# Root-mean-square factors of the two latents computed with tokens on partitions

## The chip, the cores and the metric

The kernel runs on one core of a Trainium2 chip. The metric is the device time of one launch in microseconds. Three runs of the kernel before gave 1781.26, 1781.75 and 1782.9 us, so the median is 1781.75 us.

## The reference

A decoder trunk of two layers works on 256 tokens with 2048 features, in float32. Layer one is a causal pooling mixer and a SwiGLU feed-forward block (FFN, 5632 hidden features); layer two is multi-head latent attention (16 heads) and another FFN; a root-mean-square norm (RMSNorm) ends it. What the change touches is the low-rank part of the attention:

```
y  = x * rsqrt(mean(x*x) + eps) * gain            # rms_norm
kv = rms_norm(x, kv_in_norm) @ w_kv_a             # 512 latent + 64 rotary features
c_kv = rms_norm(kv[..., :512], kv_latent_norm)    # then @ w_kv_b: keys, values of 16 heads
k_pe = apply_rope(kv[..., 512:], cos, sin)
q  = rms_norm(rms_norm(x, attn_norm) @ w_q_a, q_latent_norm) @ w_q_b   # 512 latents, 16 heads
```

Two norms follow each other here: the norm of x gives one factor per token (the same for q and kv, since only the gains differ), and each latent has a norm of its own over its 512 features.

## The kernel before

Activations lie transposed in the on-chip memory: features on the 128 partitions, the 256 tokens along the free dimension. x is 16 tiles of 128x256. Each weight is float32 and comes in by DMA in chunks of 512 to 704 KB (`raw`, 8 slots). ScalarE (ACT) copies a chunk to the rounded type fp32r (`w_hi`), VectorE (DVE) writes the rest (`w_lo`), and TensorE (PE) multiplies: for each 128x128 weight tile one matmul of `w_hi` with 512 columns (the high and low halves of the activations side by side) and one of `w_lo` with the 256 high columns (`product3`, lines 404 and 405). The kpe stage and the heads use three matmuls of 256 columns (`product_one`, lines 412 to 414).

The order of every engine's work is written out by hand. Each engine runs its own program, in order, and they meet only at semaphores. Along x there is no norm factor in the matmul operand: the operand is x times the gain, and the factor of each token is applied behind the matmul. The attention's low-rank part is these stages on PE:

- **qa**, four tiles (m = 0 to 3) of 16 weight tiles each, operand `xg`: the query latent. After m = 0, `sum_over_partitions(2)` sums the squares of x over the partitions: a matmul of an all-ones 128x128 matrix with `square_sum` (float32, 256 columns), so that each partition gets the sum of each token. ACT takes the root of the 128x256 result (`root_of`, line 820), DVE its reciprocal (`rstd_of`, line 1203).
- **kva**, four tiles, operand `xk`: the key/value latent. After m = 1, `sum_over_partitions(3)` does the same for the squares of the query latent.
- **kpe**, one tile: the shared rotary key. Between its weight tiles 7 and 8, `latent_stats` sums the squares of the key/value latent (lines 568 and 570).
- **heads**, eight pairs of heads; the first query projections follow kpe at once, the first key projection waits for the key/value latent.

For each pair of latent tiles DVE adds the two halves of the product (`lat_add`, line 1359, into `sums`), multiplies by x's factor `rstd` (`lat_scale`, line 1365, into `lat_raw`), and GpSimd (POOL) squares it and adds it up (`latent_squares`, lines 1630 and 1631). DVE itself squares the last pair of the key/value latent (lines 1419 and 1420). When the factor of the latent norm is there (`lat_rstd_of`, line 1369), DVE multiplies the four tiles by it (`lat_norm`, line 1376), ACT writes gain times that as the high half (`lat_split`, line 963) and DVE the low half (line 1381). `key_scale` (line 1427) multiplies the rotary key by x's factor; it stands between the two multiplications of `lat_norm`. ACT's four partition swaps (`rope_swap`, line 995) and `rope_cos` (line 1456) on DVE then free the PSUM bank that the first key projection writes.

Of the kernel before, what the change touches and what calls it, by code (L numbers as in the profile page):

```python
# [142 lines left out]
def trunk(nc, xT, positions, consts, bands, gains, pool_w, w_kv_a, w_k_pe, w_q_a, w_kv_k, w_kv_v, w_q_nope, w_q_pe,  # L143
          w_o, w_gate, w_up, w_down, w_last, final_gain, out):
    with ExitStack() as ctx:
# [51 lines left out]
        lat_rstd = at("lat_rstd", [P, SEQ], F32, scratch_at + 6 * KB)  # L197
# [71 lines left out]
        lat_sum = sem("lat_sum")  # L269
# [40 lines left out]
        KV, Q = 0, 1  # L310
        INIT = 4
# [88 lines left out]
        def _(pe):  # L400
# [58 lines left out]

            pe.wait_ge(init_ready, INIT)  # L460
# [92 lines left out]
            for m in range(LT):  # L553
                long_tile(CHUNK["qa"] + 2 * m, TILE["qa"] + m, xg, TILES,
                          each=(lambda kt: pe.wait_ge(xg_ready, DT + kt + 1)) if m == 0 else None)
                if m == 0:
                    sum_over_partitions(2)

            for m in range(LT):
                long_tile(CHUNK["kva"] + 2 * m, TILE["kva"] + m, xk, TILES,  # L560
                          each=(lambda kt: pe.wait_ge(xg_ready, 2 * DT + kt + 1)) if m == 0 else None)
                if m == 1:
                    sum_over_partitions(3)
            def latent_stats():

                pe.wait_ge(squares_added, squares_before(5))
                pe.wait_ge(root_ready, 4)
                pe.matmul(ps[:, STATS, 0:SEQ], ones[:, :], square_sum[:, :], start=True, stop=False)
                pe.wait_ge(pair_squared, 1)
                pe.matmul(ps[:, STATS, 0:SEQ], ones[:, :], lat_square[:, 0, :], start=False,  # L570
                          stop=True).then_inc(stats_summed, 1)

            long_tile(CHUNK["kpe"], TILE["kpe"], xk, TILES, each=lambda kt: latent_stats() if kt == TILES else None,
# [222 lines left out]
        def _(sc):  # L796
# [161 lines left out]

            def lat_split(which, number, col):
                for t in range(LT):  # L960
                    if t % 2 == 0:
                        sc.wait_ge(lat_scaled, 2 * number + t // 2 + 1)
                    nc.scalar.activation(latent[:, which, t, 0:SEQ], lat_raw[:, t, :], ACT.Identity,
# [3 lines left out]
            for w in range(3):  # L967
                split(n0 + w + SPLIT_SLOTS)
                xk_some(2)
                if w == 1:  # L970
                    root_of(3, D_MODEL)
            lat_pair("qa", 0)
            for w in range(3, 7):
                split(n0 + w + SPLIT_SLOTS)
                xk_some(2)
# [7 lines left out]
            root_of(4, LATENT)  # L983
# [14 lines left out]
            root_of(5, LATENT)  # L998
# [160 lines left out]
        def _(ve):  # L1159
# [192 lines left out]
            def lat_add(name, m):  # L1352
# [4 lines left out]
                if m > 0:  # L1357
                    ve.wait_ge(lat_sum, 1 if name == "qa" else 3)
# [431 lines left out]
```

## Time and profile before

| | |
|---|---|
| median of three runs | 1781.75 us |
| profiled execution | 1783.35 us |
| its span | 1781.4 us |
| PE busy | 1766.1 us (99%) |
| DVE busy | 1137.8 us (64%) |
| ACT busy | 915.5 us (51%) |
| POOL busy | 113.2 us (6%) |
| granted TensorE clock, mean | 0.999 of full speed |
| stages qa, kva, kpe and the first pair of heads | about 780 to 850 us |

The span runs from the first to the last instruction of one execution that the hardware profiler recorded; busy time is the time in which an engine had an instruction running. PE counts matmuls and PEld the weight loads, which overlap them. All times below are microseconds from the start of the span.

### The profile page before, as it was taken

The numbers are of one execution on the slowest core, as the hardware profiler recorded it, in microseconds if no ns is written. First come the engines' busy times: TensorE is split into PE (matmuls) and PEld (weight loads), VectorE is DVE, ScalarE is ACT, GpSimd is POOL, SyncE is SP. The second block draws the span as 40 slices with busy tenths as digits, with TensorE's granted clock in tenths as the row PEclk, the third lists the DMA queues.
The fourth block names the chain that finished last, engine by engine and source line by source line (L and its number), as shares of the span: only waits on it lengthen the run. The fifth ranks groups of instructions, "written<-read, shape, count | busy, mean of one in ns | idle before, by whom it ended". The sixth has DMA issues, their size and how long they took to land.

```text
span 1781.4 us, 29177 instructions
## 1 busy us (share of the span) xinstructions
PE 1766.1 (99%) x10376; PEld 1562.5 (88%) x10376; DVE 1137.8 (64%) x1456; ACT 915.5 (51%) x1176; POOL 113.2 (6%) x129
## 2 busy tenths in 40 slices
PE   9999999999999999999999999999999999999998
PEld 5888888888888888888999888888888888888886
DVE  4866666556666666668997776666655566666553
ACT  5766664334444444455775456666533344445433
POOL 2200000000000001123112420000000000000000
PEclk9999999999999999999999999999999999999999
DMA  6555557545555566544444555555665455556641
GB/s 250 198 190 189 190 189 238 193 158 173 188 188 188 188 224 199 174 152 138 142 154 154 189 189 188 189 188 188 221 204 177 156 189 188 190 190 223 225 147 71
DMA packets 85008, 328.26 MB, mean 184 GB/s; under 512 B 9568, under 2 KB 10336, under 8 KB 84832
## 3 DMA queue, kind: packets, MB, share of 16 engines
q1 hardware_dynamic: 84816, 326.57, 54.6%
q10 hardware_dynamic: 144, 1.05, 0.1%
q8 instruction: 30, 0.49, 0.1%
q14 instruction: 18, 0.15, 0.0%
HBM read 325.48 MB, written 2.10 MB: 184 GB/s over the span
## 4 chain that ended last, share of the span: by engine, by line
PE 97%; DVE 2%; ACT 0%; DMA 0%; issue 0%; POOL 0%; SPq 0%; ACTq 0%; POOLq 0%; DVEq 0%
PE ps L404 57%; PE ps L405 30%; PE ps L475 2%; PE ps L412 1%; PE ps L413 1%; PE ps L414 1%; PE ps L765 1%; PE ps L763 1%; PE ps L764 1%; DMA raw<-pool_w 0%; DVE w_lo L1199 0%; PE ps L598 0%; PE ps L599 0%; PE ps L600 0%; POOL square_sum L1672 0%
## 5 line engine op out<-in xcount | busy, mean ns | idle before, releaser
L1199 DVE TENSOR_TENSOR w_lo<-raw,w_hi 128x1024 fp32r<-128x1024 f32 (+2 forms) x564 | 737.5, 1309 | 421.0 <-ACT w_hi L814 418.7
L404 PE MATMUL ps<-xg,w_hi 128*128 128x512 f32 x2880 | 999.5, 390 | 0.5 <-issue 0.5
L814 ACT ACTIVATE w_hi<-raw 128x1024 fp32r<-128x1024 f32 (+2 forms) x565 | 632.0, 1120 | 552.5 <-PE ps L405 538.2
L405 PE MATMUL ps<-xg,w_lo 128*128 128x256 f32 x2880 | 812.1, 282 | 0.0
L404 PEld LDWEIGHTS ps<-xg,w_hi 128*128 128x128 f32 x2880 | 540.4, 188 | 113.8 <-issue 0.6
L405 PEld LDWEIGHTS ps<-xg,w_lo 128*128 128x128 f32 x2880 | 544.3, 189 | 0.1
L404 PE MATMUL ps<-act,w_hi 128*128 128x512 f32 x1320 | 458.0, 390 | 0.0
L405 PE MATMUL ps<-act,w_lo 128*128 128x256 f32 x1320 | 372.2, 282 | 0.0
L404 PEld LDWEIGHTS ps<-act,w_hi 128*128 128x128 f32 x1320 | 247.7, 188 | 51.9
L405 PEld LDWEIGHTS ps<-act,w_lo 128*128 128x128 f32 x1320 | 249.5, 189 | 0.0
L1279 DVE TENSOR_TENSOR sums<-ps,cross 128x512 f32<-128x512 f32 x88 | 60.9, 692 | 95.5 <-ACT cross L891 95.5
L891 ACT ACTIVATE cross<-ps 128x512 f32<-128x512 f32 x88 | 52.6, 598 | 120.6 <-PE ps L405 120.5
L404 PE MATMUL ps<-heads,w_hi 128*128 128x512 f32 x256 | 89.1, 391 | 0.0
L1630 POOL TENSOR_TENSOR square<-x 128x256 f32 (+1 forms) x32 | 33.2, 1039 | 765.2 <-DVE x L1300 765.2
L405 PE MATMUL ps<-heads,w_lo 128*128 128x256 f32 x256 | 72.2, 282 | 0.0
L1299 DVE TENSOR_TENSOR x<-ps,x 128x256 f32 (+1 forms) x76 | 32.1, 422 | 54.9 <-PE ps L405 54.9
L1283 DVE TENSOR_TENSOR sums<-sums,rstd 128x512 f32<-128x512 f32 x88 | 60.9, 692 | 3.0
L894 ACT ACTIVATE gate_act<-sums 128x256 f32<-128x256 f32 x88 | 36.8, 418 | 46.0 <-DVE sums L1283 45.8
L826 ACT ACTIVATE xg<-x,gain 128x256 fp32r<-128x256 f32 (+1 forms) x48 | 23.4, 508 | 66.5 <-DVE x L1300 62.1
L404 PEld LDWEIGHTS ps<-heads,w_hi 128*128 128x128 f32 x256 | 48.1, 188 | 9.9
L405 PEld LDWEIGHTS ps<-heads,w_lo 128*128 128x128 f32 x256 | 48.4, 189 | 0.0
L412 PE MATMUL ps<-latent,w_hi 128*128 128x256 f32 x160 | 45.2, 283 | 2.5 <-DVE gate_act L1456 2.3
(196 smaller groups left out, 1227.7 us busy)
## 6 DMA issues: line engine op xcount, KB each, us to landing
raw<-w_gate SPq DMA_DIRECT2D x176, 512.0 KB, 3.2
raw<-w_up SPq DMA_DIRECT2D x176, 512.0 KB, 3.2
raw<-w_down SPq DMA_DIRECT2D x120, 704.0 KB, 4.1
raw<-w_o SPq DMA_DIRECT2D x32, 512.0 KB, 3.2
raw<-w_last SPq DMA_DIRECT2D x11, 512.0 KB, 3.2
raw<-pool_w SPq DMA_DIRECT2D x8, 512.0 KB, 12.0
raw<-w_q_a SPq DMA_DIRECT2D x8, 512.0 KB, 3.3
raw<-w_kv_a SPq DMA_DIRECT2D x8, 512.0 KB, 3.2
```

What stands on the lines that cost most here:

```text
L404: pe.matmul(ps[:, bank, :], w_hi[:, s, j * P:(j + 1) * P], moving, start=start, stop=False)
L405: return pe.matmul(ps[:, bank, 0:SEQ], w_lo[:, s, j * P:(j + 1) * P], moving[:, 0:SEQ], start=False, stop=stop)
L412: pe.matmul(dst, w_hi[:, s, j * P:(j + 1) * P], moving[:, 0:SEQ], start=start, stop=False)
L475: mm = pe.matmul(ps[:, 4 + 2 * (g % 2) + s, :], x_pool[:, GT * g + kt, s * P:(s + 1) * P], raw[:, c, j * GT * P:(j + 1) * GT * P], start=( ...
L814: nc.scalar.activation(dst, src, ACT.Copy).then_inc(hi_ready, 1)
L891: nc.scalar.activation(cross[:, :, :], ps[:, bank:bank + 2, SEQ:], ACT.Copy).then_inc(cross_ready, 1)
L894: nc.scalar.activation(gate_act[:, :], sums[:, 0, :], ACT.Silu).then_inc(gate_ready, 1)
L1199: nc.vector.tensor_tensor(lo, src, hi.bitcast(F32), ALU.subtract).then_inc(lo_ready, 1)
L1279: nc.vector.tensor_tensor(sums[:, :, :], ps[:, bank:bank + 2, 0:SEQ], cross[:, :, :], ALU.add).then_inc(evacuated, 2)
L1283: nc.vector.tensor_tensor(sums[:, :, :], sums[:, :, :], r, ALU.mult).then_inc(sums_ready, 1)
L1299: step(nc.vector.tensor_tensor(xd, ps[:, b, 0:SEQ], xd, ALU.add))
L1630: step(nc.gpsimd.tensor_tensor(square[:, :], src, src, ALU.mult))
```

## The change

Three things change. The sums over the partitions are turned round: the squares are now the stationary operand (a 128x128 slice, so that tokens come out on the partitions) and two columns of ones the moving one (`token_sums`), for each half of the tokens. The root and the reciprocal are taken of two columns (`tok`), and PE writes the factors back to all partitions by multiplying a column, repeated 128 times as the stationary operand, with the identity (`spread`). And `lat_scale` is gone: the latents stay unscaled until `lat_norm`, whose factor is now the product of x's factor and the latent's. The root of a latent's norm is taken with x's factor squared over 512 as its scale (`X_SCALE`), one activation for each half of the tokens. ACT copies x's spread factor from PSUM to `rstd` for the rotary key. `spread` stands in PE's order in front of weight tile 8 of qa's tile 1, of weight tile 8 of kva's tile 2, and of weight tile 13 of kpe. The first pair of the key/value latent now stays in `sums`.

```diff
@@ -194,7 +194,7 @@
         lat_raw = at("lat_raw", [P, LT, SEQ], F32, scratch_at)
-        lat_rstd = at("lat_rstd", [P, SEQ], F32, scratch_at + 6 * KB)
+        tok = at("tok", [P, 9, 2], F32, scratch_at + 6 * KB)
         lat_square = at("lat_square", [P, 2, SEQ], F32, scratch_at + 4 * KB)
@@ -266,7 +266,10 @@
         pos_landed = sem("pos_landed")
-        lat_sum = sem("lat_sum")
+        tok_squared = sem("tok_squared")
+        lat_root = sem("lat_root")
+        spread_done = sem("spread_done")
+        rstd_copied = sem("rstd_copied")
         lat_scaled = sem("lat_scaled")
@@ -308,6 +311,16 @@
         KV, Q = 0, 1
+        X_ROOT, X_RSTD, X_SCALE, LAT_TOK = 0, 1, 2, 3
+        def lat_pair_of(which, m):
+            return sums[:, :, :] if (which, m) == (KV, 0) else lat_raw[:, m:m + 2, :]
+        def lat_tile_of(which, t):
+            return sums[:, t, :] if which == KV and t < 2 else lat_raw[:, t, :]
         INIT = 4
@@ -456,6 +469,23 @@
+            def token_sums(k, parts):
+                for s in range(2):
+                    for n, part in enumerate(parts):
+                        mm = pe.matmul(ps[:, STATS, 2 * s:2 * s + 2], part[:, s * P:(s + 1) * P], ones[:, 0:2],
+                                       start=(n == 0), stop=(n == len(parts) - 1))
+                mm.then_inc(stats_summed, 1)
+            def spread(k, row):
+                pe.wait_ge(rstd_ready, k)
+                for s in range(2):
+                    mm = pe.matmul(ps[:, STATS, SEQ + s * P:SEQ + (s + 1) * P],
+                                   tok[:, row, s:s + 1].broadcast_to([P, P]), const[:, C_IDENT:C_IDENT + P],
+                                   start=True, stop=True)
+                mm.then_inc(spread_done, 1)
@@ -551,26 +581,44 @@
             for m in range(LT):
-                long_tile(CHUNK["qa"] + 2 * m, TILE["qa"] + m, xg, TILES,
-                          each=(lambda kt: pe.wait_ge(xg_ready, DT + kt + 1)) if m == 0 else None)
+                def each_qa(kt, m=m):
+                    if m == 0:
+                        pe.wait_ge(xg_ready, DT + kt + 1)
+                    if (m, kt) == (1, TILES):
+                        spread(3, X_RSTD)
+                long_tile(CHUNK["qa"] + 2 * m, TILE["qa"] + m, xg, TILES, each=each_qa)
                 if m == 0:
-                    sum_over_partitions(2)
+                    pe.wait_ge(squares_added, squares_before(3))
+                    pe.wait_ge(root_ready, 2)
+                    token_sums(3, (square_sum,))
             for m in range(LT):
-                long_tile(CHUNK["kva"] + 2 * m, TILE["kva"] + m, xk, TILES,
-                          each=(lambda kt: pe.wait_ge(xg_ready, 2 * DT + kt + 1)) if m == 0 else None)
+                def each_kva(kt, m=m):
+                    if m == 0:
+                        pe.wait_ge(xg_ready, 2 * DT + kt + 1)
+                    if (m, kt) == (2, TILES):
+                        spread(4, LAT_TOK + 2)
+                long_tile(CHUNK["kva"] + 2 * m, TILE["kva"] + m, xk, TILES, each=each_kva)
                 if m == 1:
-                    sum_over_partitions(3)
-            def latent_stats():
-                pe.wait_ge(squares_added, squares_before(5))
-                pe.wait_ge(root_ready, 4)
-                pe.matmul(ps[:, STATS, 0:SEQ], ones[:, :], square_sum[:, :], start=True, stop=False)
-                pe.wait_ge(pair_squared, 1)
-                pe.matmul(ps[:, STATS, 0:SEQ], ones[:, :], lat_square[:, 0, :], start=False,
-                          stop=True).then_inc(stats_summed, 1)
-            long_tile(CHUNK["kpe"], TILE["kpe"], xk, TILES, each=lambda kt: latent_stats() if kt == TILES else None,
+                    pe.wait_ge(squares_added, squares_before(4))
+                    pe.wait_ge(root_ready, 3)
+                    pe.wait_ge(rstd_copied, 1)
+                    token_sums(4, (square_sum,))
+            def each_kpe(kt):
+                if kt == TILES:
+                    pe.wait_ge(squares_added, squares_before(5))
+                    pe.wait_ge(root_ready, 4)
+                    pe.wait_ge(lat_root, 1)
+                    pe.wait_ge(lat_scaled, 2)
+                    pe.wait_ge(pair_squared, 1)
+                    token_sums(5, (square_sum, lat_square[:, 0, :]))
+                if kt == TILES + 5:
+                    spread(5, LAT_TOK + 5)
+            long_tile(CHUNK["kpe"], TILE["kpe"], xk, TILES, each=each_kpe,
                       product=product_one)
@@ -956,11 +1004,19 @@
+            def lat_root_of(number):
+                sc.wait_ge(stats_summed, 4 + number)
+                sc.wait_ge(tok_squared, 1)
+                for s, done in enumerate((lat_root, root_ready)):
+                    nc.scalar.activation(tok[:, LAT_TOK + 3 * number, s:s + 1], ps[:, STATS, 2 * s:2 * s + 1], ACT.Sqrt,
+                                         bias=eps[:, :], scale=tok[:, X_SCALE, s:s + 1]).then_inc(done, 1)
             def lat_split(which, number, col):
...
                         sc.wait_ge(lat_scaled, 2 * number + t // 2 + 1)
-                    nc.scalar.activation(latent[:, which, t, 0:SEQ], lat_raw[:, t, :], ACT.Identity,
+                    nc.scalar.activation(latent[:, which, t, 0:SEQ], lat_tile_of(which, t), ACT.Identity,
                                          scale=gain[:, col + t, :]).then_inc(lat_hi, 1)
@@ -968,8 +1024,13 @@
                 if w == 1:
-                    root_of(3, D_MODEL)
+                    sc.wait_ge(stats_summed, 3)
+                    sc.wait_ge(rstd_ready, 2)
+                    nc.scalar.activation(tok[:, X_ROOT, :], ps[:, STATS, 0:4:2], ACT.Sqrt, bias=eps[:, :],
+                                         scale=1.0 / D_MODEL).then_inc(root_ready, 1)
             lat_pair("qa", 0)
+            sc.wait_ge(spread_done, 1)
+            nc.scalar.activation(rstd[:, :], ps[:, STATS, SEQ:], ACT.Copy).then_inc(rstd_copied, 1)
             for w in range(3, 7):
@@ -980,7 +1041,7 @@
             split(n0 + 11 + SPLIT_SLOTS)
-            root_of(4, LATENT)
+            lat_root_of(0)
             lat_split(Q, 0, G_LQ)
@@ -995,7 +1056,7 @@
-            root_of(5, LATENT)
+            lat_root_of(1)
@@ -1354,32 +1415,31 @@
                 ve.wait_ge(cross_ready, crossed[0])
-                if m > 0:
-                    ve.wait_ge(lat_sum, 1 if name == "qa" else 3)
-                nc.vector.tensor_tensor(sums[:, :, :], ps[:, t % 4:t % 4 + 2, 0:SEQ], cross[:, :, :],
+                which = Q if name == "qa" else KV
+                nc.vector.tensor_tensor(lat_pair_of(which, m), ps[:, t % 4:t % 4 + 2, 0:SEQ], cross[:, :, :],
                                         ALU.add).then_inc(evacuated, 2)
...
-            def lat_scale(m):
-                r = rstd[:, :].rearrange("p (o t) -> p o t", o=1).broadcast_to([P, 2, SEQ])
-                nc.vector.tensor_tensor(lat_raw[:, m:m + 2, :], sums[:, :, :], r, ALU.mult).then_inc(lat_sum, 1)
             def lat_rstd_of(number):
-                ve.wait_ge(root_ready, 4 + number)
-                nc.vector.reciprocal(lat_rstd[:, :], root[:, :]).then_inc(rstd_ready, 1)
-                ve.wait_ge(rstd_ready, 4 + number)
+                k, row = 4 + number, LAT_TOK + 3 * number
+                ve.wait_ge(lat_root, number + 1)
+                ve.wait_ge(root_ready, k)
+                step(nc.vector.reciprocal(tok[:, row + 1, :], tok[:, row, :]))
+                nc.vector.tensor_tensor(tok[:, row + 2, :], tok[:, row + 1, :], tok[:, X_RSTD, :],
+                                        ALU.mult).then_inc(rstd_ready, 1)
...
-                r = lat_rstd[:, :].rearrange("p (o t) -> p o t", o=1).broadcast_to([P, 2, SEQ])
+                r = ps[:, STATS, SEQ:].rearrange("p (o t) -> p o t", o=1).broadcast_to([P, 2, SEQ])
+                ve.wait_ge(spread_done, 2 + number)
                 for m in (0, 2):
-                    nc.vector.tensor_tensor(lat_raw[:, m:m + 2, :], lat_raw[:, m:m + 2, :], r,
-                                            ALU.mult).then_inc(lat_scaled, 1)
+                    pair = lat_pair_of(which, m)
+                    nc.vector.tensor_tensor(pair, pair, r, ALU.mult).then_inc(lat_scaled, 1)
                     beside[m // 2]()
...
                     nc.vector.scalar_tensor_tensor(
-                        latent[:, which, t, SEQ:], lat_raw[:, t, :], gain[:, col + t, :],
+                        latent[:, which, t, SEQ:], lat_tile_of(which, t), gain[:, col + t, :],
                         latent[:, which, t, 0:SEQ].bitcast(F32), ALU.mult, ALU.subtract).then_inc(lat_ready, 1)
@@ -1391,14 +1451,16 @@
                 if w == 1:
-                    rstd_of(3)
+                    ve.wait_ge(root_ready, 3)
+                    nc.vector.reciprocal(tok[:, X_RSTD, :], tok[:, X_ROOT, :]).then_inc(rstd_ready, 1)
+                    ve.wait_ge(rstd_ready, 3)
+                    nc.vector.scalar_tensor_tensor(tok[:, X_SCALE, :], tok[:, X_RSTD, :], 1.0 / LATENT,
+                                                   tok[:, X_RSTD, :], ALU.mult, ALU.mult).then_inc(tok_squared, 1)
             lat_add("qa", 0)
-            lat_scale(0)
             for w in range(3, 7):
...
             lat_add("qa", 2)
-            lat_scale(2)
             split(n0 + 7 + SPLIT_SLOTS)
@@ -1409,13 +1471,10 @@
             ve.wait_ge(lat_ready, LT)
-            lat_scale(0)
             split(n0 + 12 + SPLIT_SLOTS)
...
             lat_add("kva", 2)
-            lat_scale(2)
-            ve.wait_ge(lat_sum, 4)
             step(nc.vector.tensor_tensor(lat_square[:, :, :], lat_raw[:, 2:, :], lat_raw[:, 2:, :], ALU.mult))
@@ -1424,6 +1483,7 @@
                 ve.wait_ge(chunks_used, CHUNK["kpe"] + 2)
+                ve.wait_ge(rstd_copied, 1)
                 nc.vector.tensor_tensor(key_raw[:, :], ps[:, TILE["kpe"] % 4, 0:SEQ], rstd[:, :],
@@ -1652,11 +1712,11 @@
-            def latent_squares(k, number):
+            def latent_squares(k, which, first):
                 start_sum(k)
                 for d in range(SQUARED[k - 1]):
-                    gp.wait_ge(lat_sum, 2 * number + d // 2 + 1)
-                    add_square(k, lat_raw[:, d, :], d)
+                    gp.wait_ge(evacuated, first + d // 2 * 2 + 2)
+                    add_square(k, lat_tile_of(which, d), d)
@@ -1673,11 +1733,11 @@
             stream_squares(2, "down1")
-            latent_squares(3, 0)
+            latent_squares(3, Q, TILE["qa"])
...
             step(nc.gpsimd.memset(kpe[:, 1:, :].bitcast(F32), 0.0))
-            latent_squares(4, 1)
+            latent_squares(4, KV, TILE["kva"])
             n = CHUNK["qa"] + 16 + SPLIT_SLOTS
```

## Rows read from the trace of the kernel before

**Rows 1.** The page: busy time by engine, and the chain that ended last, by engine.
```profile
PE 1766.1 (99%) x10376; PEld 1562.5 (88%) x10376; DVE 1137.8 (64%) x1456; ACT 915.5 (51%) x1176; POOL 113.2 (6%) x129
...
PE 97%; DVE 2%; ACT 0%; DMA 0%; issue 0%; POOL 0%; SPq 0%; ACTq 0%; POOLq 0%; DVEq 0%
```

**Rows 2.** Waits of PE from 780 to 850: line, releaser, us, times, longest.
```profile
PE ps L412 <- DVE gate_act L1456: 1.6, 1, 1.6
PE ps L570 <- DVE lat_square L1420: 0.4, 1, 0.4
PE ps L404 <- DVE xk L1209: 0.3, 1, 0.3
```

**Rows 3.** Timeline of PE at the first sum: start us, us, engine, line, what.
```profile
786.18 0.28 PE L405 MATMUL ps<-xg,w_lo 128*128 128x256 f32 x1
...
786.97 0.28 PE L405 MATMUL ps<-xg,w_lo 128*128 128x256 f32 x1
...
789.52 0.39 PE L404 MATMUL ps<-xg,w_hi 128*128 128x512 f32 x1
```

**Rows 4.** Timeline of PE, 19.5 to 22: two-column sums in the pooling layer.
```profile
20.44 0.50 PE L483 MATMUL ps<-ones,x_square 128*128 128x2 f32 x4
20.81 1.53 PE L475 MATMUL ps<-raw,x_pool 128*128 128x512 f32 x3
```

**Rows 5.** Timeline of ACT and of DVE behind them: root and reciprocal.
```profile
20.98 0.26 ACT L872 ACTIVATE tok_root<-ps,eps 128x2 f32<-128x2 f32 x1 [4.58 <-PE ps L483]
...
21.38 0.17 DVE L1248 RECIPROCAL tok_rstd<-tok_root 128x2 f32<-128x2 f32 x1 [3.81 <-ACT tok_root L872]
```

**Rows 6.** Timeline of ACT: the root of x's norm in stage qa.
```profile
789.73 0.47 ACT L820 ACTIVATE root<-ps,eps 128x256 f32<-128x256 f32 x1
```

**Rows 7.** Timeline of PE: the hole in kva's first tile.
```profile
808.47 0.28 PE L405 MATMUL ps<-xk,w_lo 128*128 128x256 f32 x1
...
808.99 0.50 PE L404 MATMUL ps<-xk,w_hi 128*128 128x512 f32 x1 [0.25 <-DVE xk L1209]
```

**Rows 8.** Timelines of PE, ACT and DVE at the second sum, in kva.
```profile
815.00 0.59 PE L456 MATMUL ps<-square_sum,ones 128*128 128x256 f32 x2
...
816.64 0.47 ACT L820 ACTIVATE root<-ps,eps 128x256 f32<-128x256 f32 x1
...
817.99 1.75 DVE L1369 RECIPROCAL lat_rstd<-root 128x256 f32<-128x256 f32 x1
```

**Rows 9.** Timeline of PE in kpe and at the first key projection.
```profile
829.34 0.59 PE L568 MATMUL ps<-square_sum,ones 128*128 128x256 f32 x2
830.37 0.70 PE L570 MATMUL ps<-lat_square,ones 128*128 128x256 f32 x2 [0.44 <-DVE lat_square L1420]
...
831.03 0.28 PE L413 MATMUL ps<-xk,w_hi 128*128 128x256 f32 x1
...
837.80 0.27 PE L414 MATMUL ps<-latent,w_lo 128*128 128x256 f32 x1
839.64 0.36 PE L412 MATMUL ps<-latent,w_hi 128*128 128x256 f32 x1 [1.57 <-DVE gate_act L1456]
```

**Rows 10.** Timeline of DVE beside it.
```profile
828.15 0.98 DVE L1365 TENSOR_TENSOR lat_raw<-sums,rstd 128x512 f32<-128x512 f32 x1
...
833.40 1.14 DVE L1376 TENSOR_TENSOR lat_raw<-lat_raw,lat_rstd 128x512 f32<-128x512 f32 x1
834.47 0.41 DVE L1427 TENSOR_TENSOR key_raw<-ps,rstd 128x256 f32<-128x256 f32 x1
834.80 0.68 DVE L1376 TENSOR_TENSOR lat_raw<-lat_raw,lat_rstd 128x512 f32<-128x512 f32 x1
```

**Rows 11.** Timeline of ACT and of POOL beside it.
```profile
829.60 1.06 ACT L814 ACTIVATE w_hi<-raw 128x1024 fp32r<-128x1024 f32 x1 [1.31 <-PE ps L414]
...
834.58 1.84 ACT L963 ACTIVATE latent<-lat_raw,gain 128x256 fp32r<-128x256 f32 x4 [2.99 <-DVE lat_raw L1376]
...
831.59 2.41 POOL L1665 TENSOR_TENSOR w_lo<-raw,w_hi 128x1024 fp32r<-128x1024 f32 x1 [3.00 <-DVE w_lo L1199]
```

## The prediction

> **What bounds the kernel.** I read the page first: PE is busy for 1766.1 us of a span of 1781.4, and the chain of work that ended last lies on PE for 97% of its length [rows 1]. So nothing that DVE, ACT or POOL saves counts unless PE waits for it, and every matmul added to PE's order counts in full. The next view was PE's waits from 780 to 850, the stretch that holds all edited code [rows 2]: 1.6 us before a matmul of `product_one` that reads `latent`, 0.4 at the last sum, 0.3 at an `xk` tile. Then I took the real size of each hole from the timeline of PE, because a hole also costs a restart. An undisturbed pair of a 512-column and a 256-column matmul takes 0.347 us (from the second matmul at 786.97 to the first one at 789.52 lie seven pairs and 0.12 [rows 3]), so the second begins 0.23 after the first. The holes:
> - kva's first tile: the next matmul was due 0.12 after 808.47 and came at 808.99, 0.40 late, and its pair 0.11 late again: 0.51 [rows 7].
> - the last sum: from 829.34 to 831.03 where 0.12 would do, 1.57 in all. Two sums at 0.44 each (below) are 0.87 of it, the hole is 0.70 [rows 9].
> - first key projection: due at 837.92, came at 839.64: 1.72 [rows 9].
> All that a faster chain beside PE could give is 0.51 + 0.70 + 1.72 = 2.93 us, 0.16% of the time. Rows for another 1700 us belong to code that isn't touched.
>
> **The sums.** Each sum before is one float32 matmul of 256 columns, recorded as two passes. At qa it moved the next `w_lo` matmul from 786.53 to 786.97: 0.44 us [rows 3]. There are four (qa, kva, and two in kpe): 1.76 us. The two-column form runs in the pooling layer already: two matmuls in four passes, from 20.44 to 20.81, 0.37 us [rows 4], which is the loading of weights. The new kernel has this unit once in qa, once in kva and twice in kpe (two parts): 4 x 0.37 = 1.48. PE gains 0.28 us, 0.07 at each unit.
> For a weight load the Trainium skill (TensorE: Matmul & The Clock Gate, LDWEIGHTS) has columns divided by 1.2, so 107 ns for 128; this case's four passes took 0.37, that is 93 ns each [rows 4]. By the page the sums would be 16 x 0.107 = 1.71, and PE would gain 0.05 instead of 0.28. The row decides.
>
> **The spreads.** Three times two float32 matmuls of 128 columns: as many columns, passes and width of result as one old sum, 0.44 each. No row has a column repeated 128 times as stationary operand. From below the unit can't be under the four loads of 0.37 [rows 4]; from above I take 0.8, the old sum and the 0.37 one after another, if loads and columns didn't overlap. I take 0.44, since there are the same 256 columns. Three are 1.32 us of new PE work.
>
> **Waits of the first spread.** It stands eight pairs behind the sum, which is 0.37 + 2.78 = 3.15 us after the sum's start at 786.30 (0.12 after 786.18 [rows 3]): 789.45. What it waits for: ACT starts the root at 789.73 [rows 6], behind work of its own that the change leaves. The root of two columns takes 0.26, the reciprocal starts 0.14 behind it and takes 0.17 [rows 5]. So the factor is there at 789.73 + 0.26 + 0.14 + 0.17 = 790.30, and PE starts some 0.1 later, at 790.4. PE stands for 0.95 us, and 0.1 for the restart as in [rows 7]. All later work of qa queues behind this on PE. Nothing here is hidden. Before, no PE instruction waited for x's factor at this place. Bounds: 0.5 if DVE and ACT come earlier, 1.4 if each of the four hand-overs (PE to ACT to DVE to PE) costs 0.1 more.
>
> **The second spread.** Let T be the start of the sum in kva (815.00 before [rows 8]). PE is at the spread at T + 3.15. ACT starts the roots at 816.64 = T + 1.64 as before, two of 0.26 end at T + 2.16; DVE though still splits a weight chunk and is free at 817.99 = T + 2.99 only [rows 8]. Reciprocal and product, 0.17 each, with a wait between, end at T + 3.4, and PE starts at T + 3.5: a stall of 0.37 and 0.1 of restart. Bounds: 0 to 0.9.
>
> **The hole in kva's first tile.** PE comes there 0.95 + 0.1 + 0.44 - 0.07 = 1.42 later. DVE's chain to the last xk tiles starts at PE's end of qa, so it moves too, but it has lost a `lat_scale` in between, 0.68 for a 128x512 operation (as at 834.80 [rows 10]). The hole of 0.51 goes. Bounds: 0 to 0.51 is regained.
>
> So PE arrives at the half of kpe later by 1.42 - 0.51 - 0.07 + 0.37 + 0.1 + 0.44 = 1.75 us.
>
> **From kpe's half to the first key projection.** Call PE's arrival there A (829.34 before), and count from A in both kernels.
> - The last squares came late because `lat_scale` (828.15, 0.98) stood ahead of them [rows 10]. Without it the sum of squares is ready 1.02 earlier, at A + 0.01: the hole of 0.70 goes. The sums take 0.74.
> - ACT splits a chunk from A + 0.26 to A + 1.32 [rows 11], then takes two roots: A + 1.8. DVE's split now ends before that. Reciprocal and product: A + 2.3. PE reaches the spread at A + 0.74 + 5 x 0.35 = A + 2.49: no wait. It ends at A + 2.93.
> - `lat_norm` starts at A + 3.1 (833.40 = A + 4.06 before [rows 10]) and its first half is done at A + 3.8. But `key_scale` is next in DVE's order, and it waits for the end of kpe on PE: A + 2.93 + 3 x 0.35 + 0.28 = A + 4.26. It takes 0.41, the second half 0.68, so that ends at A + 5.4. Before: 835.48 = A + 6.14.
> - ACT's last two high halves take 0.9 more: A + 6.28, against 834.58 + 1.84 = 836.42 = A + 7.08 before [rows 11]. From there a weight split, four swaps and `rope_cos` are unchanged, 3.22 us to PE's restart at 839.64. PE's restart is 0.8 us earlier against A.
> The chain is tied to PE's end of kpe now; the cheap reciprocal (0.17 for 1.75 [rows 5, 8]) buys 0.8 and not 1.6 + 1.02.
>
> The first half of `lat_norm` took 1.14 instead of 0.68 while POOL was splitting a chunk from 831.59 for 2.41 us [rows 10, 11]. The Trainium skill (GPSIMD Engine Reference, Specifications) says that DVE shares its path to the on-chip memory with POOL where a DVE operation has two inputs there, and the new one takes its factor from PSUM. The trace agrees as far as the slow row goes. By the rule the first half ends at A + 3.8, without it at A + 4.25, and key_scale waits until A + 4.26 either way: the sum is the same.
>
> **The sum.** 1.75 - 0.8 = +0.95 us. Behind the first heads no instruction changes. The profiled execution took 1783.35 us, so the changed kernel's would be 1784.3; this execution was 1.6 us above the median of the runs, 1781.75, which gives 1782.7 us.
>
> **The rivals.** One bound comes first: a difference below 0.2% (3.6 us) can't be told from none in this kernel, whose three runs differ by 1.6 us.
> 1. The chain opens fully. POOL and DVE are relieved, both early spreads meet a ready factor, and key_scale doesn't hold the chain. Price: spreads 1.32, sums -0.28, holes -0.51 - 0.70 - 1.72 at best: -1.9 us, 1779.9. For it: all three holes end in work that shrinks [rows 2]. Against: ACT's root doesn't start before 789.73, 0.28 behind PE's arrival, whatever it takes [rows 6], and ACT's swaps end the longest hole.
> 2. Spreads stall and nothing is given back at the end: key_scale, standing behind a wait for PE, holds the second half longer, so that the 0.8 isn't gained and half the kva hole stays. Price: 1.75 + 0.25 + 0 = +2.0, 1783.8. For it: PE's order and DVE's order wait for each other twice within 5 us.
> 3. The two-column hand-overs are slow at PE's head (the slower side). Place: the three spreads. If each small root and reciprocal cost what the 256-column ones do (0.47 and 1.75), each factor comes 1.8 us later, the third spread waits too, and PE stands 1.8, 1.8 and 4.1 - 2.49 = 1.6 us longer than in the forecast; the last comes before the end of kpe, which the end chain is tied to, so it counts too: 0.95 + 5.2 = +6.2, 1787.9. The 0.47 and 1.75 are those at 816.64 and 817.99 [rows 8]. It decides from about 1.2 us more per spread. For it: nothing else is between PE and these factors. Against: the small ones measured 0.26 and 0.17 [rows 5].
> 4. The change doesn't do what it says for lack of a bound: sums and spreads cost the same as before on PE and no wait moves. That is 1782 within a few tenths, and indistinguishable from the forecast.
>
> **Chances.** Forecast 0.55, rival 1 0.15, rival 2 0.14, rival 3 0.07, rival 4 0.09. All but rival 3 are within 0.2%. With something for what no row shows, faster by more than 0.2% has 0.03, slower 0.07, the rest 0.90. The range must hold the cases to 2.0 above and 1.9 below and the scatter of the median, which is about a microsecond each way: 1779.8 to 1785.8.
>
> **What would show it.** Right: a wait of PE of about 1 us at the first spread with DVE's reciprocal as releaser, one of 0.4 at the second, none at the third; no wait for `xk` or `lat_square`; the wait before the first key projection still there at about 1.3 us (9.45 after A, with PE due 0.4 sooner than before); spreads of 0.44. Wrong: a stall at the third spread, a first spread without a wait, a spread over 0.8, or a key projection that starts without waiting. A time outside 1778.2 to 1785.3 would mean that something away from 780 to 850 changed, and then the whole argument from PE's waits fails.

## The result, and the profile after

The changed kernel takes 1784.27 us (median of 22 runs, 1783.79 to 1786.18) against 1781.43 for the kernel before (22 runs). The ratio is 1.0015, with a 95% interval of 1.001 to 1.0021: slower by 2.8 us, inside the 0.2% within which the prediction expected it, and inside its range, but three times the +0.95 us that it summed up. The slowest of the 22 runs before (1783.28) is still faster than the fastest of the 22 after (1783.79).

Where the time went is read from PE's timeline. The stretch that is compared runs from the start of the first sum to the second matmul after the wait at the first key projection. In the kernel before it is 839.84 - 786.30 = 53.54 us, from these two rows:

```profile
786.30 0.59 PE L456 MATMUL ps<-square_sum,ones 128*128 128x256 f32 x2
...
839.84 0.28 PE L413 MATMUL ps<-latent,w_hi 128*128 128x256 f32 x1
```

The changed kernel needs 840.99 - 784.39 = 56.60, 3.06 more; that is the whole difference and a little more. (The two profiles differ by 1.9 us ahead of the stretch, in the first 42 us, where PE waits for the pooling weights; both lengths occur again in the profiles of the experiments, with and without the change, so it is not the change's doing, and stretches are compared, not positions in the span.)

First PE's waits from 780 to 850 after the change (line, releaser, us, times, longest), which answer to [rows 2]:

```profile
PE ps L485 <- DVE tok L1428: 1.7, 2, 0.9
PE ps L425 <- DVE gate_act L1516: 1.1, 1, 1.1
PE ps L485 <- DVE tok L1455: 0.6, 1, 0.6
```

L485 is the spread. All three spreads (one in each of the stages qa, kva and kpe) wait: the first for x's reciprocal (L1455), the second and the third for the two-column product (L1428). The waits for `xk` and `lat_square` are gone, and the one before the first key projection (L425) fell from 1.6 to 1.1. PE's timeline shows the holes (start, us, engine, line, what). The bracket at the end of a row has the idle time and the line that ended it; that time is counted from the modelled end of the matmul before, so the holes in this text are taken from the starts:

```profile
784.39 0.50 PE L477 MATMUL ps<-ones,square_sum 128*128 128x2 f32 x4
784.75 0.48 PE L417 MATMUL ps<-xg,w_hi 128*128 128x512 f32 x1
785.08 0.28 PE L418 MATMUL ps<-xg,w_lo 128*128 128x256 f32 x1
...
787.51 0.28 PE L418 MATMUL ps<-xg,w_lo 128*128 128x256 f32 x1
788.43 0.68 PE L485 MATMUL ps<-const,tok 128*128 128x128 f32 x4 [0.65 <-DVE tok L1455]
788.87 0.48 PE L417 MATMUL ps<-xg,w_hi 128*128 128x512 f32 x1
789.19 0.28 PE L418 MATMUL ps<-xg,w_lo 128*128 128x256 f32 x1
...
817.10 0.28 PE L418 MATMUL ps<-xk,w_lo 128*128 128x256 f32 x1
818.16 0.68 PE L485 MATMUL ps<-const,tok 128*128 128x128 f32 x4 [0.79 <-DVE tok L1428]
818.60 0.48 PE L417 MATMUL ps<-xk,w_hi 128*128 128x512 f32 x1
818.92 0.28 PE L418 MATMUL ps<-xk,w_lo 128*128 128x256 f32 x1
...
829.70 0.28 PE L427 MATMUL ps<-xk,w_lo 128*128 128x256 f32 x1
829.94 0.35 PE L477 MATMUL ps<-ones,square_sum 128*128 128x2 f32 x2
...
830.82 0.36 PE L425 MATMUL ps<-xk,w_hi 128*128 128x256 f32 x1
831.03 0.28 PE L426 MATMUL ps<-xk,w_hi 128*128 128x256 f32 x1
...
832.54 0.28 PE L427 MATMUL ps<-xk,w_lo 128*128 128x256 f32 x1
833.75 0.71 PE L485 MATMUL ps<-const,tok 128*128 128x128 f32 x4 [0.93 <-DVE tok L1428]
...
834.42 0.28 PE L426 MATMUL ps<-xk,w_hi 128*128 128x256 f32 x1
...
839.44 0.28 PE L427 MATMUL ps<-latent,w_lo 128*128 128x256 f32 x1
840.80 0.36 PE L425 MATMUL ps<-latent,w_hi 128*128 128x256 f32 x1 [1.08 <-DVE gate_act L1516]
840.99 0.28 PE L426 MATMUL ps<-latent,w_hi 128*128 128x256 f32 x1
```

The third spread was due 0.12 after 832.54 and came at 833.75: PE stood for 1.09 us where the prediction had none. DVE's timeline beside it says why:

```profile
831.72 0.17 DVE L1427 RECIPROCAL tok<-tok 128x2 f32<-128x2 f32 x1 [0.79 <-ACT tok L1012]
831.92 1.77 DVE L1428 TENSOR_TENSOR tok<-tok 128x2 f32<-128x2 f32 x1
834.50 0.69 DVE L1437 TENSOR_TENSOR sums<-sums,ps 128x512 f32<-128x512 f32 x1 [0.80 <-PE ps L485]
835.61 0.42 DVE L1487 TENSOR_TENSOR key_raw<-ps,rstd 128x256 f32<-128x256 f32 x1 [0.42 <-PE ps L427]
835.95 0.68 DVE L1437 TENSOR_TENSOR lat_raw<-lat_raw,ps 128x512 f32<-128x512 f32 x1
```

A product of two columns took 1.77 us, ten times the reciprocal of two columns (one input) just ahead of it. It ended at 833.69. And this is POOL's timeline, whose weight split ended at 831.30 + 2.38 = 833.68:

```profile
831.30 2.38 POOL L1725 TENSOR_TENSOR w_lo<-raw,w_hi 128x1024 fp32r<-128x1024 f32 x1 [11.79 <-ACT w_hi L862]
```

At the second spread the same product took 0.49 us (start 817.53) and ended at 818.02, 0.02 behind POOL's addition of squares:

```profile
816.42 1.58 POOL L1691 TENSOR_TENSOR square_sum<-square_sum,square 128x256 f32<-128x256 f32 x1
```

So the theory to test is P: the product reads two inputs from the on-chip memory (SBUF) and stands until POOL's running instruction is over. Its rivals are H, small operations that hand over through semaphores are slow whatever POOL does, and W, the spreads' place and their weight loads are what costs, and a shorter wait at a spread only reappears before the first key projection.

### The profile page after: what moved, and what is told of

It reads as the page before. It is cut to its first block, busy times and chain, and to the rows that moved or that the text cites. A ratio compares the mean times of both kernels' runs of the same rounds, so it can differ in the third digit from the quotient of the medians.

```text
span 1782.3 us, 29227 instructions
## 1 busy us (share of the span) xinstructions
PE 1766.1 (99%) x10396; PEld 1563.2 (88%) x10396; DVE 1132.0 (64%) x1455; ACT 915.7 (51%) x1179; POOL 110.2 (6%) x129
## 4 chain that ended last, share of the span: by engine, by line
PE 97%; DVE 1%; ACT 1%; issue 1%; DMA 0%; POOL 0%; SPq 0%; ACTq 0%; DVEq 0%; POOLq 0%
PE ps L417 57%; PE ps L418 30%; PE ps L505 1%; PE ps L425 1%; PE ps L427 1%; PE ps L426 1%; PE ps L812 1%; PE ps L811 1%; PE ps L813 1%; DMA raw<-pool_w 0%; PE ps L647 0%; PE ps L646 0%; PE ps L648 0%; DVE w_lo L1260 0%; POOL square_sum L1732 0%
## 5 line engine op out<-in xcount | busy, mean ns | idle before, releaser
L425 PE MATMUL ps<-latent,w_hi 128*128 128x256 f32 x160 | 45.2, 282 | 2.0 <-DVE gate_act L1516 1.8
```

Of the source, the lines that this page charges most:

```text
L425: pe.matmul(dst, w_hi[:, s, j * P:(j + 1) * P], moving[:, 0:SEQ], start=start, stop=False)
```

## The experiments

Each was timed in 11 runs beside the kernel before. The intervals of single ratios are 0.09% (1.6 us) each way, so medians that differ by less than a microsecond are not told apart by their times alone. The conclusions rest on rows, each from one profiled execution, and on the stretch as defined above (53.54 us in the kernel before, 56.60 in the changed one).

**The split of POOL held until the third spread is done.**

```diff
             gp.wait_ge(lo_ready, made(n - 1))
+            gp.wait_ge(spread_done, 3)
             split(n)
```

> The changed kernel, with GpSimd's one weight split (2.4 us) held until the third spread is done. Theory P (the two-column product of VectorE, which reads both inputs from SBUF, stands while GpSimd works in SBUF: 1.77 us under this split, 0.49 under GpSimd's add): the product before the third spread takes about 0.17 us, the third spread's stall falls from 1.1 to under 0.2 us, the time falls by 0.7 to 1.1 us against the changed kernel (1784.3). Rival H (small operations that hand over through semaphores are slow by themselves, whatever GpSimd does): the product still takes over 1 us, stall and time stay. Rival W (the placement and the weight loads are what costs): the stall shrinks, but the time moves by less than 0.3 us, since the wait before the first key projection takes it back.

Measured: 1783.11 us (before beside it 1781.49), 1.2 below the changed kernel, stretch 55.40. DVE's timeline, third spread:

```profile
831.62 0.17 DVE L1427 RECIPROCAL tok<-tok 128x2 f32<-128x2 f32 x1 [0.79 <-ACT tok L1012]
831.82 0.16 DVE L1428 TENSOR_TENSOR tok<-tok 128x2 f32<-128x2 f32 x1
```

The product takes 0.16, the wait at the third spread is gone, and 1.2 us of the stretch with it; the hole before the first key projection stayed at 1.24. That is P. H and W fall for this place.

**One input of the product in PSUM, POOL's split left beside it.**

```diff
-                step(nc.vector.reciprocal(tok[:, row + 1, :], tok[:, row, :]))
-                nc.vector.tensor_tensor(tok[:, row + 2, :], tok[:, row + 1, :], tok[:, X_RSTD, :],
+                inverse = ps[:, STATS, 8:10]
+                step(nc.vector.reciprocal(inverse, tok[:, row, :]))
+                nc.vector.tensor_tensor(tok[:, row + 2, :], inverse, tok[:, X_RSTD, :],
```

> The changed kernel, with the reciprocal of the latent factor written to PSUM, so that the two-column product has one input in PSUM and one in SBUF; GpSimd's split stays where it is, beside it. Theory P in its narrow form (two SBUF inputs are what is held): product about 0.2 us in both places, second stall from 0.94 to about 0.6, third from 1.1 to under 0.2, time 1782.8 to 1783.6. If GpSimd holds every VectorE operation: the product still takes 1.5 us or more beside the split. Rival H: no change.

Measured: 1782.77 us, stretch 55.07. DVE, then POOL, at the third spread:

```profile
831.49 0.17 DVE L1428 RECIPROCAL ps<-tok 128x2 f32<-128x2 f32 x1 [0.79 <-ACT tok L1012]
831.70 0.16 DVE L1429 TENSOR_TENSOR tok<-ps,tok 128x2 f32<-128x2 f32 x1
```

```profile
831.08 2.38 POOL L1726 TENSOR_TENSOR w_lo<-raw,w_hi 128x1024 fp32r<-128x1024 f32 x1 [11.47 <-ACT w_hi L862]
```

With POOL in the middle of the same split the product takes 0.16. So it is the second SBUF input that is held, not the engine. The second spread's stall fell from 0.94 to 0.62, the third's to nothing. The Trainium skill (GPSIMD Engine Reference, Specifications) says that VectorE contends with GpSimd for SBUF when its instruction has two inputs there; the trace agrees, in both directions: 1.77 with two, 0.16 with one.

**The product folded away.** The root is taken of sum/512 + eps times x's root squared; its reciprocal is the whole factor.

```diff
-                step(nc.vector.reciprocal(tok[:, row + 1, :], tok[:, row, :]))
-                nc.vector.tensor_tensor(tok[:, row + 2, :], tok[:, row + 1, :], tok[:, X_RSTD, :],
-                                        ALU.mult).then_inc(rstd_ready, 1)
+                nc.vector.reciprocal(tok[:, row + 2, :], tok[:, row, :]).then_inc(rstd_ready, 1)
...
-                                         bias=eps[:, :], scale=tok[:, X_SCALE, s:s + 1]).then_inc(done, 1)
+                                         bias=tok[:, X_SCALE, s:s + 1], scale=1.0 / LATENT).then_inc(done, 1)
...
-                    nc.vector.scalar_tensor_tensor(tok[:, X_SCALE, :], tok[:, X_RSTD, :], 1.0 / LATENT,
-                                                   tok[:, X_RSTD, :], ALU.mult, ALU.mult).then_inc(tok_squared, 1)
+                    nc.vector.scalar_tensor_tensor(tok[:, X_SCALE, :], tok[:, X_ROOT, :], EPS,
+                                                   tok[:, X_ROOT, :], ALU.mult, ALU.mult).then_inc(tok_squared, 1)
```

> The changed kernel without the two-column product: the root is taken of sum/512 + eps*(x's root squared), so its reciprocal is the whole factor. Theory P: the two waits lose product and hand-over: the second stall falls from 0.94 to about 0.4, the third from 1.1 to 0; time 1782.4 to 1783.2. Rival H: only the length of one operation of two goes, 0.2 us at each of two places, 1783.9. Rival W: time within 0.3 us of the changed kernel.

Measured: 1783.52 us, stretch 54.87. The second stall fell to 0.42 and the third is gone, as P has it, and the stretch is the shortest so far; but the time is 0.75 us above the kernel with the PSUM input, and misses the expectation. In the profile the excess lies elsewhere. PE has a wait of 0.44 in the head loop (due at 874.50, came at 874.94), where the changed kernel had 0.17 and the kernel before had 0.32. And from the last matmul's start to the end of the span it takes 7.8 us instead of 7.3; the rows of the computing engines in that end are as long as in the changed kernel, and the excess comes after the last of them.

**The first two spreads four weight tiles later.**

```diff
-                    if (m, kt) == (1, TILES):
+                    if (m, kt) == (1, TILES + 4):
...
-                    if (m, kt) == (2, TILES):
+                    if (m, kt) == (2, TILES + 4):
```

> The changed kernel with the first two spreads four weight tiles (1.39 us) later in TensorE's order; the product stays. Theory P and the prediction's reckoning of the waits alike: the stalls of 0.80 and 0.94 us at the first and second spread go to 0, the third keeps its 1.1, and the time falls by 1.5 to 1.9 us, to 1782.4 to 1782.8. If these waits are made good elsewhere (the hole in kva's first tile comes back with 0.5, later work waits instead): under 1.0 us is gained.

Measured: 1782.2 us, stretch 54.63, a little more gained than expected. No wait at the first two spreads (each unit costs 0.45, with the slower matmul pair behind it), 1.07 still at the third. The hole in kva's first tile did not come back. The two stalls had been paid in full: 1.97 us of the stretch, restarts included, 2.1 us of the time.

**Both repairs together**: PSUM input and later spreads.

> The changed kernel with both repairs: one input of the two-column product in PSUM, and the first two spreads four weight tiles later. Theory P: no spread waits any more; against the PSUM kernel (1782.8) the two stalls of 0.81 and 0.62 us go: 1781.3 (1780.9 to 1781.8), the time of the kernel before. What is left of the change then is three spreads with restart (1.6 us) and dearer sums in kpe, against the two holes closed and the shorter last one. Rival W: 1782.2 or more, because work behind the spreads gives the gain back.

Measured: 1781.16 us (before beside it 1781.63), ratio 0.9996 (0.9987 to 1.0005), stretch 53.47, against 53.54 before the change. The two repairs add up as expected. No spread waits any more, and the difference from the kernel before lies inside the interval: the loss is gone.

**Both repairs, and key_scale behind the second half of `lat_norm`.**

```diff
-            lat_norm(KV, 1, G_LKV, beside=(key_scale, lambda: None))
+            lat_norm(KV, 1, G_LKV, beside=(lambda: None, key_scale))
```

> As the kernel with both repairs, and key_scale (the rotary key's multiplication, which waits for TensorE's end of kpe) moved behind the second half of the latent's multiplication on VectorE. Theory K (the hole of 1.24 us before the first key projection is tied to the end of kpe through key_scale): the second half starts about 0.7 us earlier, the hole falls to 0.5 to 0.7 us, time 1780.7, below the kernel before. Rival: the hole is tied to ScalarE's own order (the split before the swaps waits for TensorE), and stays over 1 us: 1781.3.

Measured: 1780.71 us, ratio 0.9996 (0.9987 to 1.0005), stretch 52.82. PE at the first key projection:

```profile
836.26 0.28 PE L427 MATMUL ps<-latent,w_lo 128*128 128x256 f32 x1
836.98 0.36 PE L425 MATMUL ps<-latent,w_hi 128*128 128x256 f32 x1 [0.44 <-DVE gate_act L1517]
```

The hole is 0.60 instead of 1.24: it did hang on the end of kpe through key_scale. By its median this is the fastest of the kernels here, 0.9 below the one before; the interval of the ratio doesn't exclude equality.

**The same move in the kernel before.**

> The kernel before with the same move of key_scale and nothing else. There key_scale does not wait (it starts as soon as VectorE is free), so only its own 0.4 us is taken out of the chain: the hole of 1.72 falls to about 1.4, time 1781.1 to 1781.4. If it gained 0.7 us as well, what the repaired kernel wins by the move would have nothing to do with the change.

Measured: 1781.56 us, against 1781.63, stretch 53.39. The hole before the key projection shrank from 1.72 to 1.00, more than the expected 1.4, but 0.51 of that came back as a new hole at the first query projection, which waits for key_scale. The stretch gained 0.15 in all, where the same move in the repaired kernel gained 0.65. So the move is worth something only where the latent's factor comes early.

**The kernel before, with POOL's split held until the first half of the latent's multiplication.**

```diff
             gp.wait_ge(lo_ready, made(n - 1))
+            gp.wait_ge(lat_scaled, 3)
             split(n)
```

> The kernel before, with GpSimd's split held until the first half of the latent's multiplication is done. Theory P: that multiplication (128x512, two SBUF inputs) takes 0.69 instead of 1.14 us; the hole before the first key projection shrinks by up to 0.4 us, unless the split now slows the second half by as much; time 1781.0 to 1781.5. It shows whether the same hold is in the kernel before, and how much smaller it is there. Rival H: 1.14 stays.

Measured: 1784.51 us, 2.9 above the kernel before (1781.63), where a gain of 0.1 to 0.6 was expected; stretch 55.48. DVE, then POOL:

```profile
831.27 0.69 DVE L1376 TENSOR_TENSOR lat_raw<-lat_raw,lat_rstd 128x512 f32<-128x512 f32 x1
831.88 0.42 DVE L1427 TENSOR_TENSOR key_raw<-ps,rstd 128x256 f32<-128x256 f32 x1
832.22 2.93 DVE L1376 TENSOR_TENSOR lat_raw<-lat_raw,lat_rstd 128x512 f32<-128x512 f32 x1
```

```profile
832.20 2.40 POOL L1665 TENSOR_TENSOR w_lo<-raw,w_hi 128x1024 fp32r<-128x1024 f32 x1 [5.74 <-DVE lat_raw L1376]
```

The first half is freed, as P says, 0.69 for 1.14 [rows 10]. The second half started 0.02 behind POOL and took 2.93: it ended 0.55 after POOL's end at 834.60. The expectation had taken the hold for a share of the speed; it is a hold for the rest of the other instruction. PE then stood for 3.45 us (due at 835.85, came at 839.30), and when it went on the granted clock was lower. Busy time of each engine in three windows (window, length in us, then PE, PEld, DVE, ACT, POOL, the granted clock, DMA share, GB/s):

```profile
830.00:839.00 9.00, 6.01 (x52) 5.80 (x50) 8.19 (x10) 4.61 (x10) 2.40 (x1) 1.00 0.37 118
839.00:843.00 4.00, 3.70 (x19) 3.73 (x20) 1.54 (x3) 2.54 (x6) 3.35 (x4) 0.57 0.39 131
843.00:850.00 7.00, 6.98 (x60) 6.78 (x58) 5.26 (x9) 6.07 (x9) 0.74 (x1) 1.00 0.22 53
```

**Every spread issued twice**, in the kernel with both repairs.

```diff
-                for s in range(2):
+                for s in (0, 1, 0, 1):
                     mm = pe.matmul(ps[:, STATS, SEQ + s * P:SEQ + (s + 1) * P],
```

> The kernel with both repairs (one product input in PSUM, spreads four tiles later), with every spread issued twice. It prices a spread by itself. The prediction's price, 256 columns of a two-pass float32 matmul: 0.36 to 0.44 us each, with no new wait; three of them, and the third one's delay passes on to the last hole's chain: 1781.16 + 1.1 to 1.3, 1782.3 to 1782.5. If the weight loads of a repeated column were slow, over 0.8 us each and 1783.6 or more. If TensorE has slack here after all: under 0.5 us.

Measured: 1783.1 us (before beside it 1781.94), stretch 54.81. The stretch grew by 1.34, three times 0.45: PE's third spread starts at 833.35 and the next matmul at 834.16 (0.81), where a single one takes 0.36 to the next (832.45 to 832.81 in the kernel with the PSUM input). Against the kernel before beside it the time is 1.2 up, where the single one was 0.5 down: 1.6, somewhat over the 1.1 to 1.3 expected. So PE has no slack here, and a spread costs what its 256 columns were priced at: a column repeated 128 times as stationary operand is not slow.

**The product folded away, and the spreads later.**

> The changed kernel without the product (the root carries the whole factor), and the first two spreads four tiles later. By the stalls alone it should equal the other repaired kernel, 1781.2. The kernel with the product folded and early spreads was 0.7 us slower than its stalls allow, with issue gaps in the head loop and a longer end; if that comes from the program's length or place in memory, it shows here too: 1781.7 to 1782.2; if it was chance, 1781.0 to 1781.4.

Measured: 1782.27 us (before beside it 1781.94), stretch 53.47, to the hundredth that of the kernel with both repairs, and yet 0.8 us dearer when each is held against its own kernel before. It has the same wait of 0.45 in the head loop and the same long end (7.9 us) as in the other folded kernel, where the ten profiles without the fold have 7.2 to 7.3: hardly chance. What in the program brings it stays open.

## Why the prediction was right, and where it was mis-sized

The bound was right: the loss is the sum of what PE waits for and executes in 50 us of the program, and the repaired kernel gets it back without a change anywhere else. The size was not: +2.8 us lies inside the range because the range was wide, and "a stall at the third spread" is a sign that the prediction itself had named for being wrong. Its statement that a difference below 3.6 us can't be told from none came from three runs; with 22 of each, 2.8 us stands clear. By the prediction's steps, in us of the stretch (predicted, measured):

| step | predicted | measured |
|---|---|---|
| sums in qa and kva, each | 0.37 | 0.46 |
| first spread, with wait and restart | 1.49 | 1.33 |
| hole in kva's first tile | 0 | 0 |
| second spread, with wait and restart | 0.91 | 1.47 |
| sums in kpe | 0.74 | 1.09 |
| third spread | 0.44 | 1.64 |
| hole before the first key projection | 1.3 | 1.24 (1.31 with restart) |

With the restart counted, the measured column adds up to 7.76 (the sums of qa and kva twice). The same places cost 4.76 in the kernel before, so 3.00 of the 3.06 are accounted for.

- **The first spread's wait** was right in place and size: 0.80 for 0.95, with DVE's reciprocal as releaser. The kernel with later spreads shows that it was paid in full. What the prediction doesn't say is why this factor is late: ACT spends 1.28 us on a table load right in front of the root (in the kernel before too, at 788.44), and none in front of the two later ones.

```profile
786.53 1.28 ACT L1029 ACT_TABLE_LOAD   x1
```

- **The hole at xk and the hole at `lat_square`** went as reckoned, the second but for a start of the sums in kpe that was 0.12 late.
- **"Reciprocal and product: A + 2.3. PE reaches the spread at A + 2.49: no wait"** is the step that failed, 1.2 us of the missing 2.1. A, PE's arrival at the half of kpe, is 829.82 here. The reciprocal ended at 831.89 = A + 2.07, in time; the product was priced at 0.17, the price of a neighbour with one input, and took 1.77. The prediction had the port rule in hand and weighed it for `lat_norm` only, where it changed nothing, and not for the smallest instruction of the chain, which reads two SBUF inputs beside the same POOL split. The size of the held instruction says nothing about the hold, which lasts until POOL's instruction ends.
- **The second spread** was 0.56 over. 0.32 is the product (0.49 for 0.17; the kernel with the PSUM input gives back just 0.32). The rest is DVE's split ahead of it, 1.58 instead of 1.23, less 0.09 by which PE came later itself. Without `lat_scale` POOL's squares of the key/value latent start at 815.72, right there, where before they started at 823.60. POOL was slowed as well: its addition of squares took 1.58 beside that split and 0.74 at 818.77. That this is the same hold is read from these rows (DVE, then POOL); no run tested it by itself.

```profile
815.83 1.58 DVE L1260 TENSOR_TENSOR w_lo<-raw,w_hi 128x1024 fp32r<-128x1024 f32 x1 [0.26 <-ACT w_hi L862]
815.72 0.61 POOL L1690 TENSOR_TENSOR square<-sums 128x256 f32<-128x256 f32 x1 [0.80 <-DVE sums L1419]
818.77 0.74 POOL L1691 TENSOR_TENSOR square_sum<-square_sum,square 128x256 f32<-128x256 f32 x1
```

- **The two-column sums** cost more than in the pooling layer: 0.46 (from 784.39 the second matmul was due at 784.62, it came at 785.08), not less than the old 0.44 [rows 3], and in kpe 1.09 for eight passes. The saving of 0.28 on PE was a loss of 0.26. In qa the unit itself took 0.36, as in [rows 4]; 0.1 came on top in the pair of matmuls behind it (0.33 from the first to the second instead of 0.23), which the price from [rows 4] leaves out. Whether the change from float32 back to fp32r matmuls causes that was not tested. In kpe the four sums took 0.22 each, and 0.12 is the late start.
- **The end chain** was right in its mechanism. key_scale was the wait (0.42 for PE's last kpe matmul, at 835.61), and the hole was there with 1.24; the move of key_scale showed the tie.

Of the rivals, the nearest to what happened is the third in its form, hand-overs slow at PE's head, with 1.6 us more at the spreads than forecast instead of its 5.2, and a cause that it didn't name: the small root and reciprocal kept their 0.26 and 0.17, as it said against itself. The second rival's time (1783.8) is the nearest to the measured one by chance: the hole in kva's first tile was gone and the last hole had its forecast size, so what it describes did not happen.

## What to carry to other kernels

Before a small VectorE operation is put on a chain that TensorE waits for, look at what GpSimd runs at that moment: with two SBUF inputs it can cost nearly as much as GpSimd's whole instruction (1.77 of 2.38 us here), and with one input in PSUM it cost 0.16 us. Give a round trip TensorE to ScalarE to VectorE to TensorE the 3.9 to 4.2 us that the first two took here, by placing its consumer later in TensorE's order; twelve weight tiles instead of eight removed two stalls at no cost. And a cheaper operation off the critical engine is no gain until the added matmuls, with their restarts, are paid: here three spreads at 0.45 us used up all that the relieved VectorE could give back.

## What the runs showed that was not expected

- A VectorE operation with two SBUF inputs that meets a running GpSimd instruction waits for its end: 128x2 elements took 1.77 us and ended 0.01 us behind GpSimd; 128x512 took 2.93 and ended 0.55 behind it; in the kernel before, 1.14, ending at 834.54, 0.54 behind GpSimd's end at 834.00 [rows 10, 11].
- After TensorE had stood for 3.45 us (busy for 6.01 us of 9.00), its granted clock averaged 0.57 in the next 4 us, most of it at the lower level of 1.2 GHz, and matmuls of 256 columns took 0.41 instead of 0.28. The stall of 1.24 us in the changed kernel left it at 1.00 (839.5 to 843).
- A change of a few instructions in the programs of VectorE and ScalarE (the folded product) went with a longer time in code that it didn't touch, in both kernels that had it: some 0.5 us more from the stretch's end to the last matmul (934.5 us, 934.0 in the changed kernel), and half a microsecond more from there to the end of the span. The cause is open.
